# Taps of a convolution moved from the w_in_2 to the w_out products of a fused two-block kernel

## The reference, cut to what matters

```python
u = _rmsnorm(h, mix_norm_g)
p = u @ w_in                                  # 1024 -> 1792
p_pool, p_bval, p_bgate, p_cgate, p_cx = jnp.split(p, [256, 512, 768, 1280], axis=-1)
y_a = _pool_mixer(p_pool, pool_w, pool_scale)        # windowed means, then 4 small matmuls of 64x64
y_b = _conformer_conv(p_bval, p_bgate, ...)          # v * sigmoid(gate), a causal depthwise convolution
                                                     # of 31 taps, layernorm, silu, 256x256 matmul
y_c = _rglru_branch(p_cgate, p_cx, ...)              # conv of 4 taps, two gates, a linear scan, gelu gate
h = h + jnp.concatenate([y_a, y_b, y_c], axis=-1) @ w_out
# then rmsnorm, MLP with squared relu, residual, final rmsnorm
```

## Time and profile before

| | |
|---|---|
| median of 3 runs | 1064.41 us (1064.27 to 1066.69) |
| profiled execution, its own time | 1065.81 us |
| its span, first to last instruction | 1064.0 us |
| mean granted TensorE clock | 0.985 |
| TensorE busy | 1024.9 us, 96% |
| VectorE busy | 507.4 us, 48% |
| ScalarE busy | 422.3 us, 40% |
| GpSimd busy | 574.1 us, 54% |
| HBM traffic | 98.61 MB, 93 GB/s mean |

### The profile page before, as it was taken

One profiled execution on the slowest core, in us unless ns is written; L12 is line 12 of the kernel. 1 busy time (PEld: TensorE's weight loads), 2 busy tenths in 40 slices (PEclk: granted clock), 3 DMA queues, 4 the chain that ended last, 5 costly groups with the idle time before them and its releaser, 6 DMA issues.

```text
span 1064.0 us, 12498 instructions
## 1 busy us (share of the span) xinstructions
PE 1024.9 (96%) x4959; PEld 859.4 (81%) x4959; DVE 507.4 (48%) x828; ACT 422.3 (40%) x657; POOL 574.1 (54%) x712
## 2 busy tenths in 40 slices
PE   6999999999999999999999779999999999999996
PEld 5888888888888888888898667888788888888884
DVE  2781356665356633545677984366113213212332
ACT  5353445555624424433345573353222212212231
POOL 3555546556556755465634777364645554555540
PEclk9999999999999999999999898999999999999998
DMA  6223222122442215232312202322323232322312
GB/s 220 85 82 117 79 79 81 45 74 80 145 133 79 79 50 202 88 119 80 119 54 67 79 20 79 99 80 79 119 79 115 84 119 80 108 90 79 119 40 79
DMA packets 91403, 98.61 MB, mean 93 GB/s; under 512 B 3234, under 2 KB 86720, under 8 KB 91344
## 3 DMA queue, kind: packets, MB, share of 16 engines
q1 hardware_dynamic: 91344, 97.81, 28.4%
HBM read 95.71 MB, written 2.10 MB: 92 GB/s over the span
## 4 chain that ended last, share of the span: by engine, by line
PE 86%; DVE 6%; POOL 3%; ACT 2%; issue 2%; DMA 0%; SPq 0%; DVEq 0%; POOLq 0%
PE ps L321 78%; POOL wlo L245 2%; POOL tmp L1130 1%; PE ps L663 1%; PE ps L644 1%; PE ps L788 1%; DVE ps L1112 1%; DVE Hl L428 1%; PE ps L601 1%; PE ps L603 1%; DVE tmp L1534 1%; DVE tmp L406 1%; PE ps L366 1%; PE ps L395 0%; ACT Hh L427 0%
## 5 line engine op out<-in xcount | busy, mean ns | idle before, releaser
L245 POOL TENSOR_TENSOR wlo<-raw,whi 128x256 fp32r<-128x256 f32 x672 | 513.4, 796 | 407.1 <-ACT whi L240 407.1
L321 PE MATMUL ps<-Hh,whi 128*128 128x512 f32 x848 | 337.0, 397 | 2.7 <-ACT whi L240 1.9
L321 PE MATMUL ps<-Hl,whi 128*128 128x512 f32 x848 | 333.2, 393 | 0.0
L240 ACT ACTIVATE whi<-raw 128x1024 fp32r<-128x1024 f32 x168 | 177.2, 1056 | 174.6 <-PE ps L321 169.4
L321 PE MATMUL ps<-Hh,wlo 128*128 128x512 f32 x848 | 213.1, 390 | 0.0
L321 PE MATMUL ps<-Ah,whi 128*128 128x512 f32 (+1 forms) x576 | 197.9, 366 | 2.6 <-DVE Fm L1096 2.0
L321 PE MATMUL ps<-Al,whi 128*128 128x512 f32 (+1 forms) x576 | 195.2, 361 | 0.0
L321 PEld LDWEIGHTS ps<-Hh,whi 128*128 128x128 f32 x848 | 161.2, 190 | 37.5 <-ACT whi L240 2.1
L321 PEld LDWEIGHTS ps<-Hl,whi 128*128 128x128 f32 x848 | 161.1, 190 | 33.3 <-issue 0.5
L321 PEld LDWEIGHTS ps<-Hh,wlo 128*128 128x128 f32 x848 | 159.8, 188 | 33.5
L321 PE MATMUL ps<-Ah,wlo 128*128 128x512 f32 (+1 forms) x576 | 124.3, 361 | 0.0
(11 more groups left out here) (269 smaller groups left out, 908.6 us busy)
## 6 DMA issues: line engine op xcount, KB each, us to landing
raw<-in_w_in SPq DMA_DIRECT2D x36, 1024.0 KB, 5.3
raw<-in_w_up SPq DMA_DIRECT2D x16, 1024.0 KB, 5.3
raw<-in_w_down SPq DMA_DIRECT2D x16, 1024.0 KB, 5.0
raw<-in_w_att_out SPq DMA_DIRECT2D x4, 1024.0 KB, 5.0
raw<-in_w_sg_out SPq DMA_DIRECT2D x4, 1024.0 KB, 4.9
raw<-in_w_o SPq DMA_DIRECT2D x4, 1024.0 KB, 5.0
Fm<-in_x SPq DMA_DIRECT2D x2, 1024.0 KB, 6.2
Fm<-in_x SPq DMA_DIRECT2D x1, 2048.0 KB, 8.1
```

What stands on the lines that cost most here:

```text
L240: eh = A(lambda e, s=s, src=src, kk=kk: e.activation(wtile(whi, s, kk), src, ACT.Copy), raw_ev[b], used)
L245: el = G(lambda e, s=s, src=src, kk=kk, cut=cut: e.tensor_tensor(wtile(wlo, s, kk)[:, *cut], src[:, *cut], f(wtile(whi, s, kk))[:, *cut], ...
L321: return e.matmul(ps[:, bk, 0:c1 - c0], wt, x[:, k, c0:c1], start=st, stop=sp)
```

## The change

Only the order inside `mixers` changes. `rg_scan(1)` goes one step later, behind `conv_input(1)`. Calls of `taps` are taken out of, or made smaller in, steps 12 to 23, and added in later ones. `rg_input(3)` goes one step later. `pool_out(0)` goes from step 28 to 29, `pool_out(1)` from 30 to 31, and each is asked for in the middle of a w_out product and not in front of one; `pool_low(1)` no longer stands behind `pool_out_low(0)`. The last taps and `conv_merge` go to step 34 (32 and 33 before), `conv_sums` from step 35 to 36. `conv_norm` stays at 37 and `conv_mix` at 39. The calls of `side_taps` stay at their steps.

```diff
--- before.py
+++ after.py
@@ -1319,33 +1319,27 @@
             yield
             taps(2, (0,))
             rg_scan(0)
+            table(ACT.Sigmoid)
+            yield
+            conv_input(1, *made[5])
             rg_scan(1)
-            table(ACT.Sigmoid)
-            yield
-            conv_input(1, *made[5])
-            taps(3, (0,))
             yield
             side_taps()
-            taps(3, (1,))
-            taps(1)
+            taps(2, (1,))
             yield
             cx(2, *made[6])
             taps(1)
             rg_conv(2)
-            taps(1)
             rg_low(2)
             yield
             side_taps()
-            taps(2)
             yield
             cx(3, *made[7])
             taps(1)
             rg_conv(3)
-            taps(1)
             rg_low(3)
             yield
             side_taps()
-            taps(2)
             yield
             rg_gate(2, 0)
             scale_cg(0)
@@ -1353,7 +1347,7 @@
             yield
             rg_gate(2, 1)
             side_taps()
-            taps(2)
+            taps(1)
             yield
             rg_gate(3, 0)
             scale_cg(1)
@@ -1362,15 +1356,15 @@
             yield
             rg_gate(3, 1)
             rg_exps(2)
-            taps(2)
+            taps(1)
+            yield
+            scale_cg(2)
             rg_input(3)
-            yield
-            scale_cg(2)
             side_taps()
             taps(1)
             rg_root(2)
             yield
-            taps(2)
+            taps(1)
             rg_scan(2)
             rg_scan(3)
             gelus((0, 1, 2))
@@ -1388,30 +1382,30 @@
             yield
             es = pool_low(0, ea)
             side_taps()
+            yield
+            ea = pool_mix(1, *made[9])
+            es1 = pool_low(1, ea)
+            yield
+            e5 = pool_out(0, es)
+            side_taps()
+            pool_out_low(0, e5)
+            taps(2)
+            yield
             taps(1)
             yield
-            ea = pool_mix(1, *made[9])
-            e5 = pool_out(0, es)
-            taps(1)
-            pool_out_low(0, e5)
-            es = pool_low(1, ea)
-            yield
-            side_taps()
-            taps(2)
-            yield
-            e5 = pool_out(1, es)
+            e5 = pool_out(1, es1)
             taps(1)
             pool_out_low(1, e5)
             yield
             taps(2)
             yield
+            taps(3)
+            yield
             taps(N_DVE)
-            yield
             merged = conv_merge()
             yield
             yield
             sp = conv_sums(*merged)
-            yield
             yield
             cn = conv_norm(sp)
             yield
```

More of the change, by code:

```diff
@@ L1321, in mixers @@
             rg_scan(0)
-            rg_scan(1)
             table(ACT.Sigmoid)
@@ L1325, in mixers @@
             conv_input(1, *made[5])
-            taps(3, (0,))
+            rg_scan(1)
             yield
             side_taps()
-            taps(3, (1,))
-            taps(1)
+            taps(2, (1,))
             yield
@@ L1364, in mixers @@
             rg_exps(2)
-            taps(2)
-            rg_input(3)
+            taps(1)
             yield
             scale_cg(2)
+            rg_input(3)
             side_taps()
```

## The result

| | before | after |
|---|---|---|
| median, 8 runs each | 1068.55 us | 1060.47 us |
| range | 1064.27 to 1069.38 | 1058.35 to 1063.33 |
| ratio, 95% interval | | 0.9948 (0.9930 to 0.9965) |
| the same kernel once more, 12 runs | | 0.9962 (0.9944 to 0.9981) |
| profiled execution, its span | 1065.81, 1064.0 | 1063.24, 1061.5 |

0.9948 of 1064.41 is 5.5 us less, with an interval of 3.7 to 7.5; the prediction's 1055.6 is 8.8 less. The direction was right, the size was not. The ratio is not that of the two medians, which differ by 8.1 us (0.9924): five of the eight executions before lie between 1068.53 and 1069.38, the other three between 1064.27 and 1066.69. Four other sets of executions of the kernel before, 16 to 29 each, have medians of 1064.36 to 1065.75, and the kernel after, run again beside one of them, is 4.0 us faster by the medians.

The account below looks back on a forecast made before the run. VectorE was taken to stand behind TensorE's gaps, 18.7 us between 525 and 690 us. The walk through its queue gave a shift of 8.8 us and no tail waits: 1064.41 to 1055.6 us, range 1050 to 1060.5.

Parts of the forecast that it names:

- Part 1: Scan behind conv_input(1): VectorE's L1096 starts earlier, so TensorE's wait ending at 576.63 loses 1.97 us.
- Part 2: Fewer taps in steps 12 to 16: gate (2,1) moves from 599.27 to 592.0; shift 9.0 us by step 20.
- rg_conv(3) runs 586.1 to 588.5: On VectorE, ahead of gate (2,1): rg_conv(3) ends at 588.5 against 595.8, 7.3 us earlier.
- I take the clock held here too: At gate (2,1): a wait of 2.0 us leaves the clock up, saving 1.75 us on the matmuls behind.
- Part 3: Pool's matmuls in the w_out products: pool_low(1) done at 637.1 against 646.8; nothing counted for the moved matmuls' waits.
- Part 4: 18 taps in w_out at 0.66 us each: third w_out product starts at 651.3 against 660.11, shift 8.8 us.
- Part 5: Convolution's tail: no wait before the sums, by 0.5 us, nor before their spread, by 0.6 us.
- the clock rival: Slow matmuls after gate (2,1) and in the third w_out product add 3.4 us, giving 1059; chance 0.14.
- the clock takes back more: Rival: two more unhidden slow stretches, after gate (2,1) and in the third w_out product, give 1059; chance 0.14.
- VectorE is less in the way: Rival: half of VectorE's idle time in parts 2 and 4 goes, 4 to 5 us more, 1051; chance 0.13.
- margins gone: Rival, convolution's tail: merge or chain late by 2 us each, plus a slow stretch, 1061; chance 0.08.
- slower: Rival: w_out taps beside POOL cost 1.31 us each against 0.66, giving 1068; decides from 1.15 per tap; chance 0.05.

Follow-up runs that it names:

- one fill: The changed kernel with 14 unread matmuls in one wait: before gate (2,1), 0.9955 of the kernel before; or for pool_out_low(1), 0.9945.
- both: The changed kernel with 14 unread matmuls in each of two waits, before gate (2,1) and for pool_out_low(1), and conv_sums in two halves: 0.9945 of before.
- the split sums: The changed kernel with the 32 one-column matmuls of conv_sums in two halves, in the middle of and behind the third w_out product: 0.9960 of before.
- the best version: The changed kernel with unread matmuls in two waits, conv_sums halved, and side taps of steps 15 and 17 at 30 and 31: 0.9925 of before.

## Why the prediction was wrong in size

**Part 1** held: no wait stands there after. But its 1.97 us are no term of their own: without part 2 they move on to cx(2), as the run with the scan alone showed. In the walk they were used only together, so the sum is not hurt.

**Part 2 is the step that failed, in two terms.** "rg_conv(3) runs 586.1 to 588.5" took three L1026 at their price with POOL idle. The new order put them beside POOL's L1130, and they took 3.68. The row for this was there, 2.87 us for the same three before, and I priced the moved taps beside POOL and not the instructions that the taps' departure moved. It made gate (2,1) 1.0 late, and deferring POOL's sums gave 0.92 of that back. The Trainium skill (SBUF — State Buffer, "Who interferes with whom") says that VectorE and GpSimd share one pair of ports, and that a VectorE instruction with two SBUF inputs and a GpSimd one that reads SBUF exclude each other. The runs agree in which instructions suffer (L1026, L1139, L1166 with two SBUF inputs; not L1112, whose accumulator is in PSUM). The mean price of one L1026 went from 0.79 to 1.23 us, but it is no fixed one: the first of the three took only 0.80 beside POOL.

"I take the clock held here too" was wrong: the wait was 3.5 us, not 2.0, and the clock fell. It fell behind 2.5 us as well, with POOL's sums moved, and held behind 1.3, with the side taps moved; a wait of 2.0 at this place was never run, so whether it would have held stays open. This is the other 1.45 of the 2.47 us that are missing from gate (3,1) on. Of the 1.75 us that I counted as saved, 1.34 came back at gate (3,1) when the wait was filled, and 0.76 at the last pair product. The price itself was nearly right (1.61 in the kernel before; my "15 matmuls" are 18, six of them of half width); that it would be saved was not. It is also luck how large it comes out: in seven profiles with the same order up to there and no fill, gates (2,1) and (3,1) lie 8.4 to 9.9 us apart.

**Part 3:** nothing was counted for the moved matmuls and nothing came. The pool part took 0.7 us more than in the walk, by the instruction that stood beside POOL (1.68 for L1179 where 0.9 stood). The wait for pool_mix(0)'s bank I missed. That it cost nothing, as VectorE was later, is argued; it fits the run with pool's matmuls at their old steps, which does not have it and is no faster.

**Part 4** was right: 18 taps at 0.66. x1_add came 3.16 us after the predicted offset, which is what parts 2 and 3 owe (2.47 and 0.7). Behind it my walk stopped looking at TensorE, and this is the next term that failed. The 22 matmuls behind the wait for pool_out_low(1) took 8.0 us and not 5.0, ended 1.4 us after VectorE had freed the first bank, and made the third product 4.6 late.

**Part 5:** both margins held, no wait stood there. The slow stretch of matmuls behind the sums was longer than before and cost 1.2 us more; it appears in no part of my sum but the clock rival. Another 0.6 us went by the MLP wait: 0.3 of it in the spread's own matmuls, still slow (2.19 against 1.88), the rest not followed up.

Together 6.4 us are missing in this profile, and the stretch got 2.4 shorter instead of 8.8. About 1.7 of the 6.4 are VectorE's instructions beside POOL, about 4.1 are TensorE at 1.2 GHz, which the sum held at nothing or counted as saved. The terms are not independent (filled or moved alone, each gave less than its size at the last pair product). Over all executions the gain is 5.5 us; the profiled one is the second slowest of its eight, with the lowest mean clock, and that is as far as I can explain the difference. **The rival "the clock takes back more", with 1059 and a chance of 0.14, is the nearest to what happened**: 1064.41 x 0.9948 = 1058.9. It named the places, behind gate (2,1) and in the third product; the second was the product before it. That the number agrees within 0.1 is luck: it left out the instructions beside POOL and the sums, and took 1.7 for each fall. Of the clock gate the Trainium skill (TensorE: Matmul & The Clock Gate, Part 1) says that it follows how busy the array has been. The traces agree for the falls behind waits. At the one-column matmuls the profile shows TensorE busy all the time (4.00 of 4 us from 664 to 668 too) and the clock is lost all the same, so a full busy share in the profile doesn't by itself mean that the clock holds.

"VectorE is less in the way", "margins gone" and "slower" did not happen; the last needed 1.15 us per tap, and the taps stayed at 0.66.

**Not settled:** what each clock fall costs on average. A profile shows one execution: with one fill, both, or the split sums the stretch was 2.3 to 4.1 us shorter than after's, while the ratios, 0.9945 to 0.9960, can't be told from after's own two, 0.9948 and 0.9962. How much of the 0.2 to 0.4% between the best version and the change is real stays open too.

## What to carry to other kernels

Walk the bottleneck engine's queue through a new order with each instruction at its price beside its new neighbours, not beside the old ones, and above all the instructions that you did not move. When waits shrink but multiply, ask after each whether the engine behind it is on the critical path when the clock falls: the same 3.0 us of slow matmuls cost 1.4 where VectorE was later anyway, and all 3.0 where it was not. Removing the wait that the profile names can make things worse, if the next one stands in a more exposed place.

## What I had not expected of the hardware

A run of 32 one-column matmuls, with TensorE busy for all of 3.5 us, was accompanied or followed by a stretch at 1.2 GHz in 10 of the 12 profiles that ran them in one piece, before included (from 667 us), and in none of the four in which half a product stood between two halves of them. The two exceptions are the runs with POOL's sums later and with the kernel before filled. That the one-column matmuls are the cause is likely by this, and not shown by the times. Useless matmuls in a wait can pay: 28 of them made the kernel before 0.3% faster (0.9968, 0.9951 to 0.9986). In the kernel after, 14 in a wait of 3.5 us changed nothing that the times can tell (0.9955 against 0.9948 and 0.9962).
